# The 48 steps of the later modulation rows: one at a time, or two in a row

## The chip, the cores and the metric

The kernel runs on one core of a Trainium2 chip. The time is that of the device, in microseconds, for one launch: lower is better. A core has five engines with instruction queues of their own: TensorE (PE, its weight loads are shown as PEld), VectorE (DVE), ScalarE (ACT), GpSimd (POOL) and SyncE (SP), which here only issues transfers from the memory (HBM) into the core's SBUF. Each engine works through its instructions in the order of the program, and waits on semaphores for the others.

## The reference

One layer of a diffusion backbone: 256 latent tokens x and 256 context tokens, model width D = 2048, everything in float32.

```
mod = silu(c) @ w_mod + b_mod          # 2048 -> 6 x 2048: sh1, sc1, g1, sh2, sc2, g2
h = modulate(rms_norm(x), sh1, sc1); hc = the same for the context
p = h @ w_in; pc = hc @ w_in[:, :STATE_END]
...  # short convolutions, gated DeltaNet (8 heads, both directions) from p and pc,
...  # a Conformer convolution branch from p
x = x + g1 * rms_norm(mix @ w_out)
hf = modulate(rms_norm(x), sh2, sc2)
x = x + g2 * rms_norm((silu(hf @ w_gate) * (hf @ w_up)) @ w_down)
```

`mod` is a product of one vector with a matrix of 2048 x 12288. Its first two rows (sh1, sc1) are needed before the projections. The next three (g1, sh2, sc2) are needed only after the mixer, and they are "the later modulation rows". The last one, g2, is made on VectorE during the feed-forward part.

## The kernel before, in words

**Products.** TensorE multiplies float32 in a split form: each operand is a high part (`w_hi`) and a low part (`w_lo`), and three matmuls (high x high, high x low, low x high) make one product (helper `product`, L1775). ScalarE makes the high part by a copy (`hi` step, L921), VectorE the low part as `raw - w_hi` (`lo` step, L1355).

**Units and the ring.** Weights of the projections come in units of 128 x 1024 elements (512 KB). Each is loaded into one of four slots of `raw` (RING = 4), split into one of four slots of `w_hi` and `w_lo`, and multiplied by the `mm` step in four quarters (`QS = 4`). There are 128 units of the input projections ("win"), two small ones ("ba"), and 32 of the output projection ("wo").

**The later modulation rows.** They are worked out in 48 steps `mrm`: three row groups (MR = 3) of 16 steps (KT = 16). A step takes 128 rows of `w_mod`, 2048 columns wide, as two halves of 512 KB. Each half is loaded into a slot of the same ring `raw`, and is not split: TensorE reads it in plain float32. A step is four matmuls of 512 columns (L2083), each with one column of weights (`csil`), in four column groups of the array at once. All accumulate in PSUM bank 3. After the 16th step of a group, ScalarE copies the sums (`mrc`), and TensorE turns them (`mcol`), then VectorE adds the bias (`mcc`).

**The order of the loads.** `make_plan` writes one list of steps; every engine walks this list and does its own steps of it. At its end the list `ring` is taken from it: one entry for each `hi` step and two for each `mrm` step, in the order of the plan. Entry n uses slot n % 4. SyncE issues the loads in this order (L731), and before that of entry n it waits for the last reader of entry n - 4:

```
old = RINGED[n - RING]
if old[0] == "mr":
    need(sp, "mrm", *old[1:3])
else:
    need(sp, "hi", old)
    need(sp, "lo", old)
```

So a slot that held a modulation half is free when TensorE has done that step, and one that held a unit is free when VectorE has made its low part.

**The order around the steps.** `splits_ahead` puts the `hi` and `lo` steps of a unit two units ahead of its `mm` (AHEAD = 2). Where a level of the solver's inverse (`z`, `zc`, `xy`, `xadd`) falls into a unit, it is one unit ahead, and one more `hi` comes right behind the `zc`, one more `lo` right behind the `xadd`. In a unit, behind each quarter, the planner lays the steps of the solver, of the scan's state, of the norms and of VectorE's convolution (`dw`), by lags counted in quarters. The `mrm` steps come behind the last quarter of a unit, by the count of the units done: `gates(MR * KT * done // total - (MR * KT - len(mr)))`, with 48 steps over 108 units, so one every two or three units.

**The early rows.** The first two modulation rows are made by 32 `wm` steps in the first 127 us. They have the same shape as an `mrm` step, with two columns of weights and a buffer of their own (`first`, L1870).

Of the kernel before, what the change touches and what calls it, by code (L numbers as in the profile page):

```python
# [31 lines left out]
KT = D // P  # L32
# [29 lines left out]
MR = 3  # L62
# [105 lines left out]
def norm_chunks():  # L168

    ch = [[("lnm", ()), ("cen", ())], [("csq", (0,))]]  # L170
    ch += [[("lnv", (i,)), ("lva", (i,))] + ([("csq", (i + 1,))] if i < 3 else []) for i in range(4)]
    ch += [[("lsd", ()), ("lnr", ()), ("lnn", ())]]
    ch += [[("lny", (i,)), ("mix_hi", (NP + i,)), ("mix_lo", (NP + i,))] for i in range(4)]
    return ch


def evacuation(cu):

    what, s, p = cu
    m = NP * s + p  # L180
    if what in "kvq":
        return [("tap2", cu), ("tapa", cu)], [(AFTER["taps"][m], [("taps", cu)]), (AFTER["csilu"][m], [("csilu", cu)]), (AFTER["nat"][m], [("nat", cu), ("natc", cu)])], []
    if what == "z":
        return [("zsilu", cu)], [], []
    if what == "a":
        return [], [], []
    return [("sg", (p,)), ("u", (p,))], [], [[("dw", (p, n))] for n in range(NDW)]
# [15 lines left out]
def make_plan():  # L203
    plan = [("masks", ()), ("zero", ()), ("csil", ())]
    mr = [(grp, j) for grp in range(MR) for j in range(KT)]
# [3 lines left out]
    def put(steps):  # L209
        plan.extend(steps)  # L210
        for x in steps:
            placed[x] = slot[0]

    def unit(u, parts=1, beside=lambda: None):
        plan.extend([("hi", (u,)), ("lo", (u,))])
        for part in range(parts):
            plan.append(("mm", (u, part)))
            beside()
# [45 lines left out]
    def gates(n):  # L264
        for grp, j in mr[:n]:
            if grp and j == 0:
                plan.extend([("mcol", (grp - 1,)), ("mcc", (grp - 1,))])
            plan.append(("mrm", (grp, j)))
            if j == KT - 1:
                plan.append(("mrc", (grp,)))  # L270
        del mr[:n]
# [37 lines left out]
    done = 0  # L309
    total = 4 * (len(STREAM) - 1 - len(EARLY))  # L310
    for n, cu in enumerate(STREAM):
        if cu == ("z", LAT, NP - 1):
            gates(len(mr))
            plan.extend([("mcol", (MR - 1,)), ("mcc", (MR - 1,))])
        rest = [c[0] for c in STREAM[n:]]
        slot[2] = slot[0] + 16 * (rest.index("g") + 1 if "g" in rest else 4)
        if cu == EARLY[-1]:
            pass
        for g in range(NQ - 1 if cu in EARLY else 0, 4):
            unit(("win", cu, g), QS, beside)  # L320
            done += cu not in EARLY
            gates(MR * KT * done // total - (MR * KT - len(mr)))
            plan.extend(lat)
            del lat[:]
        now, then, later = evacuation(cu)
        put(now)
        soon += [(slot[0] + wait, steps) for wait, steps in then]
        late += later
        if cu == ("g", LAT, 3):
            late += norm_chunks()  # L330
        if n in (MIX["ba0"], MIX["ba1"]):
            s = CTX if n == MIX["ba0"] else LAT
            if cu[0] in "kvq":
                put([("taps", cu)])
                soon.remove(next(x for x in soon if x[1] == [("taps", cu)]))
            unit(("ba", s))
            put([(x, (s,)) for x in GATE_STEPS[:7]])
            soon.append((slot[0] + AFTER["gates"], [(x, (s,)) for x in GATE_STEPS[7:]]))
            soon.sort(key=lambda x: x[0])
# [80 lines left out]
def count_steps():  # L420

    plan, ring = make_plan()
    count, totals = {}, {}
    for kind, key in plan:
        assert (kind, key) not in count, (kind, key)
        totals[kind] = totals.get(kind, 0) + 1
        count[kind, key] = totals[kind]

    bank, before, reader = {}, {}, {}
    free, lent = [(6, None), (7, None)], None  # L430
    for kind, key in plan:
        if kind == "mm" and key[0][0] == "wo" and not lent:
            lent = [step for n, step in free if n == 2]
            free = [x for x in free if x[0] != 2]
            assert lent
        release = released_by(kind, key)
        if release:
            assert free, (kind, key)
            bank[kind, key], before[kind, key] = free.pop(0)
            reader[release] = bank[kind, key]  # L440
        if (kind, key) in reader:
            free.append((reader.pop((kind, key)), (kind, key)))
        if (kind, key) == ("u", (0,)):
            free.append((2, (kind, key)))
    assert not reader
    return plan, ring, count, totals, bank, before, lent[0]
# [1739 lines left out]
```

## Time and profile before

| | us |
|---|---|
| median of 3 runs | 1656.04 (1654.19 to 1660.93) |
| profiled execution, span from first to last instruction | 1654.2 |
| mean granted TensorE clock | 0.985 |
| PE busy | 1555.3 (94%) |
| DVE busy | 1043.9 (63%) |
| ACT busy | 769.0 (46%) |
| POOL busy | 226.7 (14%) |

The page of the profile gives no other time for the profiled execution than its span; the fastest of the timed runs, 1654.19 us, agrees with it. The `mrm` steps lie between 174 and 757 us. PE busy is the time covered by at least one matmul, whose ends are modelled: matmuls overlap in the records, so a matmul's own duration (0.28 us) is more than its distance to the next one (0.12 us). The distances between starts are what counts. "Idle before" in a row is the time in which the engine did nothing before the instruction, with the name of what ended it.

### The profile page before, as it was taken

The page shows a single profiled execution, that of the slowest core. Times are in us where ns is not written, and L with a number is a line of the kernel's source. Part 1 is how long each engine was busy: PE and PEld are TensorE (multiplying, and loading weights), DVE is VectorE, ACT ScalarE, POOL GpSimd, SP SyncE. Part 2 cuts the span into 40 slices and gives each one's busy share as a digit, 9 for nine tenths or more (in the row PEclk, how much of TensorE's full clock was granted, in tenths as well). Part 3 has the DMA queues.
Part 4 walks back from the last instruction along what each step waited for, and adds up shares of the span by engine and source line. Part 5 has one row for each costly group of instructions (what it writes and reads, how often), then busy time and mean ns, then how long its engine had stood idle before and what let it go on. Part 6 is the DMA issues. An engine that isn't in the chain of part 4 may idle for free.

```text
span 1654.2 us, 25093 instructions
## 1 busy us (share of the span) xinstructions
PE 1555.3 (94%) x9295; PEld 1300.8 (79%) x9295; DVE 1043.9 (63%) x1446; ACT 769.0 (46%) x1044; POOL 226.7 (14%) x236
## 2 busy tenths in 40 slices
PE   3787899998989999999998999999999999999998
PEld 0466788887879898898876888888888888888786
DVE  1445798989897957675565554444555454777554
ACT  5536543534345745456345644444444444443332
POOL 2000233323332334244200000000000000000000
PEclk9999999999999999999999999999999999999999
DMA  9994465655555556564464666666666666898653
GB/s 343 374 378 112 143 211 166 205 178 194 177 166 166 166 181 199 173 200 139 129 223 120 189 188 189 188 189 189 190 190 190 190 190 198 323 314 312 208 181 131
DMA packets 190977, 334.58 MB, mean 202 GB/s; under 512 B 14706, under 2 KB 80354, under 8 KB 189985
## 3 DMA queue, kind: packets, MB, share of 16 engines
q1 hardware_dynamic: 190194, 330.89, 62.3%
q0 software_dynamic: 688, 2.39, 0.5%
q8 instruction: 63, 1.03, 0.3%
q14 instruction: 32, 0.26, 0.1%
HBM read 331.15 MB, written 2.10 MB: 201 GB/s over the span
## 4 chain that ended last, share of the span: by engine, by line
PE 80%; DVE 10%; DMA 4%; ACT 3%; issue 2%; SPq 1%; DVEq 0%; ACTq 0%
PE PS L1775 65%; DMA first<-in_w_mod_dram 4%; DVE cacc L1636 3%; DVE w_lo L1355 2%; PE PS L1781 2%; PE PS L2083 2%; PE PS L2037 2%; PE PS L1989 2%; DVE sil L1464 1%; PE PS L1935 1%; PE PS L1870 1%; PE PS L1979 1%; DVE gh L1522 1%; DVE xyi L1527 1%; SPq L708 1%
## 5 line engine op out<-in xcount | busy, mean ns | idle before, releaser
L921 ACT ACTIVATE w_hi<-raw 128x1024 fp32r<-128x1024 f32 (+1 forms) x426 | 448.4, 1056 | 526.6 <-PE PS L1775 440.3
L1322 DVE TENSOR_TENSOR w_lo<-raw,w_hi 128x1024 fp32r<-128x1024 f32 x264 | 322.9, 1225 | 324.3 <-ACT w_hi L921 324.3
L1775 PE MATMUL PS<-w_hi,h_hi 128*128 128x512 f32 x704 | 275.0, 391 | 1.8 <-DVE h_lo L1377 1.2
L1775 PE MATMUL PS<-w_hi,h_lo 128*128 128x512 f32 x704 | 274.0, 389 | 0.0
L1775 PE MATMUL PS<-w_lo,h_hi 128*128 128x512 f32 x704 | 274.0, 389 | 0.0
L1355 DVE TENSOR_TENSOR w_lo<-raw,w_hi 128x1024 fp32r<-128x1024 f32 (+1 forms) x162 | 202.0, 1255 | 75.9 <-ACT w_hi L921 75.9
L1775 PE MATMUL PS<-h_hi,w_hi 128*128 128x256 f32 (+1 forms) x784 | 238.0, 304 | 0.8 <-ACT w_hi L921 0.8
L1775 PE MATMUL PS<-h_lo,w_hi 128*128 128x256 f32 (+1 forms) x784 | 222.1, 283 | 0.0
L1775 PE MATMUL PS<-h_hi,w_lo 128*128 128x256 f32 (+1 forms) x784 | 222.1, 283 | 0.0
L1775 PEld LDWEIGHTS PS<-h_hi,w_hi 128*128 128x128 f32 (+1 forms) x784 | 149.3, 190 | 36.9 <-issue 24.2
L1775 PEld LDWEIGHTS PS<-w_hi,h_hi 128*128 128x128 f32 x704 | 132.2, 188 | 29.5 <-DVE h_lo L1377 1.4
L1775 PEld LDWEIGHTS PS<-w_hi,h_lo 128*128 128x128 f32 x704 | 132.1, 188 | 27.6
L1775 PEld LDWEIGHTS PS<-w_lo,h_hi 128*128 128x128 f32 x704 | 132.2, 188 | 27.1
L1775 PEld LDWEIGHTS PS<-h_lo,w_hi 128*128 128x128 f32 (+1 forms) x784 | 149.6, 191 | 0.9
L1775 PEld LDWEIGHTS PS<-h_hi,w_lo 128*128 128x128 f32 (+1 forms) x784 | 149.0, 190 | 0.1
L1775 PE MATMUL PS<-w_hi,act_hi 128*128 128x512 f32 x352 | 140.4, 399 | 0.0
L1775 PE MATMUL PS<-w_hi,act_lo 128*128 128x512 f32 x352 | 139.5, 396 | 0.0
L1775 PE MATMUL PS<-w_lo,act_hi 128*128 128x512 f32 x352 | 139.5, 396 | 0.0
L1636 DVE SCALAR_TENSOR_TENSOR cacc<-ub,vcol,cacc 128x196 f32<-128x196 f32 (+14 forms) x240 | 123.9, 576 | 0.2
L870 POOL TENSOR_TENSOR mkl<-kc,lvl 128x512 fp32r<-128x512 f32 x56 | 82.4, 1471 | 158.5 <-PE PS L1979 123.8
L1775 PE MATMUL PS<-hc_hi,w_hi 128*128 128x256 f32 (+1 forms) x272 | 84.9, 312 | 12.7 <-DVE sil L1464 3.9
L1522 DVE TENSOR_TENSOR gh<-PS,side 128x1024 fp32r<-128x1024 f32 x48 | 58.5, 1219 | 43.5 <-PE PS L1989 42.5
(322 smaller groups left out, 2374.4 us busy)
## 6 DMA issues: line engine op xcount, KB each, us to landing
raw<-in_w_in_dram SPq DMA_DIRECT2D x128, 512.0 KB, 3.9
raw<-in_w_mod_dram SPq DMA_DIRECT2D x96, 512.0 KB, 4.8
raw<-in_w_gate_dram SPq DMA_DIRECT2D x88, 512.0 KB, 3.7
raw<-in_w_up_dram SPq DMA_DIRECT2D x88, 512.0 KB, 3.7
raw<-in_w_down_dram SPq DMA_DIRECT2D x88, 512.0 KB, 4.3
first<-in_w_mod_dram SPq DMA_DIRECT2D x64, 512.0 KB, 10.3
raw<-in_w_out_dram SPq DMA_DIRECT2D x32, 512.0 KB, 4.1
gin<-in_w_mod_dram SPq DMA_DIRECT2D x32, 512.0 KB, 5.8
```

The lines of the kernel that those rows point to most:

```text
L708: sp.dma_start(first[:, slot, :].rearrange("p (a b) -> p a b", a=2), w_mod_v[:, 2 * j:2 * j + 2, part * D + q * 512:part * D + (q + 1) * 5 ...
L870: pool.tensor_tensor(mkl[:, :, :, :].rearrange("p t h c -> p (t h) c"), kc[:, :, :, :].bitcast(F32).rearrange("p t h c -> p (t h) c"), bc( ...
L921: act.activation(out_ap, in_ap, ACT.Copy).then_inc(S[kind], 1)
L1322: dve.tensor_tensor(w_lo[:, slot, :], raw[:, (R0 + n) % RING, :], w_hi[:, slot, :].bitcast(F32), ALU.subtract).then_inc(S["lo"], 1)
L1355: dve.tensor_tensor(lo, raw[:, at_ring[u] % RING, 0:sz], hi.bitcast(F32), ALU.subtract).then_inc(done, 1)
L1522: dve.tensor_tensor(gh[:, :, :, :, :].rearrange("p a t h c -> p (a t h) c"), grown.rearrange("p a (n c) -> p (a n) c", c=P), bc(side[:, l, ...
L1636: ins = dve.scalar_tensor_tensor(out=dst, in0=src, scalar=vcol[:, col:col + 1], in1=dst, op0=ALU.mult, op1=ALU.add)
L1775: ins = pe.matmul(out_ap, a[i], b[j], start=start and n == 0, stop=stop and n == 2, skip_group_check=grouped)
L1781: ins = pe.transpose(PS[:, bank_, P * n:P * (n + 1)], src, ident[:, :])
L1989: ins = pe.matmul(PS[:, b, P * n:P * (n + 1)], a, m, start=False, stop=True, skip_group_check=True)
L2037: ins = pe.matmul(PS[:, b, P * n:P * (n + 1)], a, m, start=True, stop=True)
L2083: ins = pe.matmul(PS[32 * tile:32 * tile + 1, 3, :], csil[:, LAT, j:j + 1], raw[:, n % RING, 512 * h:512 * (h + 1)], start=j == 0, stop=j ...
```

## The change

The number of steps that are due after a unit is rounded to an even number: the steps are emitted two at a time, at 24 places instead of 48. The places of the second, fourth, ... step stay. The rest of the order is as it was, and so are the shapes, the buffers and the semaphores.

```
@@ -319,7 +319,7 @@
         for g in range(NQ - 1 if cu in EARLY else 0, 4):
             unit(("win", cu, g), QS, beside)
             done += cu not in EARLY
-            gates(MR * KT * done // total - (MR * KT - len(mr)))
+            gates(2 * (MR * KT // 2 * done // total) - (MR * KT - len(mr)))
             plan.extend(lat)
             del lat[:]
         now, then, later = evacuation(cu)
```

As `ring` is taken from the plan, the order of the loads follows: a pair has four entries in a row.

## Rows read from the trace of the kernel before

**Rows 1.** The page, busy time of each engine.
```profile
PE 1555.3 (94%) x9295; PEld 1300.8 (79%) x9295; DVE 1043.9 (63%) x1446; ACT 769.0 (46%) x1044; POOL 226.7 (14%) x236
```
**Rows 2.** Stretches: length, then busy PE, PEld, DVE, ACT, POOL, PEclk, DMA share, GB/s.
```profile
160.00:360.00 200.00, 186.72 (x1469) 166.49 (x1468) 176.65 (x311) 93.70 (x146) 58.43 (x53) 0.97 0.55 179
360.00:560.00 200.00, 186.62 (x1453) 166.66 (x1452) 179.76 (x296) 93.68 (x146) 63.02 (x58) 0.97 0.54 178
560.00:757.00 197.00, 192.62 (x1575) 172.95 (x1574) 131.41 (x205) 114.87 (x191) 72.68 (x75) 1.00 0.57 183
```
**Rows 3.** The page, the group of the steps' matmuls: busy, mean ns, idle before.
```profile
L2083 PE MATMUL PS<-raw,csil 128*1 128x512 f32 x384 | 51.6, 609 | 1.6 <-DMA raw<-in_w_mod_dram 1.6
```
**Rows 4.** TensorE's timeline (start, duration): steps 2, 16, 36 and 48.
```profile
188.59 1.04 PE L2083 MATMUL PS<-raw,csil 128*1 128x512 f32 x8
...
354.86 1.04 PE L2083 MATMUL PS<-raw,csil 128*1 128x512 f32 x8
...
613.17 1.04 PE L2083 MATMUL PS<-raw,csil 128*1 128x512 f32 x8
...
756.08 1.04 PE L2083 MATMUL PS<-raw,csil 128*1 128x512 f32 x8
```
**Rows 5.** TensorE's timeline around one step.
```profile
306.60 0.28 PE L1775 MATMUL PS<-h_hi,w_lo 128*128 128x256 f32 x1
306.81 1.04 PE L2083 MATMUL PS<-raw,csil 128*1 128x512 f32 x8
...
308.01 0.28 PE L1775 MATMUL PS<-h_lo,w_hi 128*128 128x256 f32 x1
```
**Rows 6.** TensorE's timeline, two early steps in a row.
```profile
71.16 1.90 PE L1870 MATMUL PS<-first,csil 128*2 128x512 f32 x16
```
**Rows 7.** SyncE's queue in the timeline, before step 16.
```profile
345.10 0.82 SPq L731 DMA_DIRECT2D raw<-in_w_mod_dram  x2
```
**Rows 8.** VectorE's timeline: low parts of the units split last before a place.
```profile
190.56 1.23 DVE L1355 TENSOR_TENSOR w_lo<-raw,w_hi 128x1024 fp32r<-128x1024 f32 x1 [0.46 <-ACT w_hi L921]
...
256.93 1.22 DVE L1355 TENSOR_TENSOR w_lo<-raw,w_hi 128x1024 fp32r<-128x1024 f32 x1
...
355.24 1.21 DVE L1522 TENSOR_TENSOR gh<-PS,side 128x1024 fp32r<-128x1024 f32 x1
356.37 1.21 DVE L1355 TENSOR_TENSOR w_lo<-raw,w_hi 128x1024 fp32r<-128x1024 f32 x1
...
381.38 1.22 DVE L1355 TENSOR_TENSOR w_lo<-raw,w_hi 128x1024 fp32r<-128x1024 f32 x1
...
753.44 1.22 DVE L1355 TENSOR_TENSOR w_lo<-raw,w_hi 128x1024 fp32r<-128x1024 f32 x1
```
**Rows 9.** The page, DMA issues: KB each, median us from issue to landing.
```profile
raw<-in_w_in_dram SPq DMA_DIRECT2D x128, 512.0 KB, 3.9
raw<-in_w_mod_dram SPq DMA_DIRECT2D x96, 512.0 KB, 4.8
```
**Rows 10.** TensorE's timeline, two idle times and what ended them.
```profile
491.70 0.84 PE L1967 MATMUL PS<-nid_r,pi 128*128 128x128 f32 x4 [2.59 <-DVE pi L1509]
...
624.04 0.66 PE L1781 MATMUL PS<-ident,sil 128*128 128x128 f32 x4 [1.42 <-ACT sil L1048]
```
**Rows 11.** Stretches behind idle times, columns as in rows 2.
```profile
249.70:256.50 6.80, 6.75 (x30) 4.92 (x31) 5.61 (x12) 1.06 (x1) 1.81 (x2) 0.50 0.67 217
...
492.00:495.50 3.50, 3.50 (x17) 3.24 (x15) 3.39 (x8) 0.00 (x0) 1.36 (x2) 0.51 0.00 0
...
624.00:627.40 3.40, 3.36 (x28) 3.27 (x29) 3.21 (x4) 3.35 (x11) 0.53 (x1) 1.00 0.20 35
```
**Rows 12.** Waits from 160 to 757 us: us in total, times, longest.
```profile
PE PS L1967 <- DVE pi L1509: 6.6, 3, 2.7
...
PE PS L1989 <- ACT pi L921: 2.5, 5, 0.8
...
ACT w_hi L921 <- DMA raw<-in_w_in_dram: 63.5, 30, 9.6
```

More of the change, by code:

```diff
@@ L321, in make_plan @@
             done += cu not in EARLY
-            gates(MR * KT * done // total - (MR * KT - len(mr)))
+            gates(2 * (MR * KT // 2 * done // total) - (MR * KT - len(mr)))
             plan.extend(lat)
```

## The prediction

> **What bounds the kernel now.** I read the busy line, then the stretches of the span, then TensorE's timeline around one step, then the DMA issues, then VectorE's timeline at the places that the change keeps. The busy line has PE at 94% [rows 1]. By stretches, PE is busy for 187 of each 200 us while the 48 modulation steps are worked in (160 to 757 us), and VectorE for 177 and 180 of 200 us up to 560 us [rows 2]. So PE sets the time, and VectorE is close behind it: whatever keeps PE waiting is paid in full, and VectorE has little room to do its work early. One core, one profiled execution: span 1654.2 us, which is 1.8 us under the median of 1656.04; I add that at the end.
>
> **The change, part by part.** Work is the same: 48 steps, 384 matmul records [rows 3], 96 loads of 512 KB. The 24 places that stay are those of the second, fourth, ... step (with 108 units counted, the j-th pair comes after unit 4.5 j rounded up, where step 2j was). The first step of each pair moves back by two or three units. I number the places 1 to 24; the first is at 188.6 us, the last at 756.1 us [rows 4].
>
> *What it saves (term A).* A step uses one column in each of four column groups of the array, the projections use all 128. Around a single step, the last matmul before starts at 306.60, the step at 306.81, and the second matmul behind it at 308.01 [rows 5]. Matmuls follow each other by 0.12 us there, so without the step that one would start at 306.84: a step costs 1.17 us. The trace of before has two such steps in a row, among the early ones: 16 records in 1.90 us against 8 in 1.04 us [rows 5, 6]. The second costs 0.86 us, which is 0.31 us less. 24 x 0.31 = 7.4 us saved, if nothing waits. Bounds: 0 (if a pair would drain between its halves, which [rows 6] exclude) and 7.4. Two smaller parts have one answer: the turning of row group 0 and 1 (mcol, mcc) moves back with the pair and has nobody waiting for it, and the copies mrc stay. Cost 0.
>
> *What it adds (term B).* The raw ring has four slots and a step takes two, each filled by a load that SyncE issues in ring order. A load may be issued only when the slot's last reader is through. Before, a step's two loads reused the slots of the step before or of the units just behind it, and were issued early: for the step at 354.86 us at 345.10 us [rows 4, 7]. Now the four loads of a pair take the whole ring. The fourth reuses the slot of the unit split last ahead of the pair, and that unit is the second one *behind* the pair on PE. So the load must wait for this unit's w_lo on VectorE (L1355), and the pair's second half waits on PE for the load. In PE's queue everything stands behind it: the projections and all the solver's matmuls.
>
> How late is that w_lo? Its end minus the place, in the trace, for the 24 places (first, last and the telling ones in between are in [rows 4, 8]): +3.2, +0.7, +0.3, -3.5, +2.7, +1.4, +1.3, +2.7, +2.0, +0.2, +1.7, +5.6, -1.5, -0.6, +2.5, -0.9, -0.3, +2.5, -2.9, 0.0, +2.5, +3.6, -1.6, -1.4 us. A load lands 3.9 us after its issue (median of the units' loads; those of the steps 4.8, since they queue in twos) [rows 9]. PE does the pair's first half meanwhile, 0.9 us. So the stall is that number + 3.0 us, where positive. It is 2 us or more at 19 of 24 places, and the sum is 93 us. PE's stalls also give VectorE and ScalarE time to catch up, so I split the 93 by what makes the w_lo late:
> - Places 8, 15, 18 and 22: in VectorE's order the w_lo stands right behind the work on the solver's last matmuls before the place (gh at 355.24, then w_lo at 356.37 [rows 8]). It is late by its position, no slack on VectorE helps. 5.7 + 5.5 + 5.5 + 6.6 = 23 us, kept in full.
> - Places 2, 9, 11, 12, 17 and 24: the same, but with one to three quarter units between. 26 us; two of them (381.38 to 382.60 at place 9 [rows 8], and place 12) carry a backlog too and are cut to 3.6 us: 20 us.
> - The other 14 (43 us, place 1 alone 6.2): the w_lo comes before the last unit in the order, and is late by backlog only. Place 4 shows it without: 256.93 to 258.15 [rows 8], 3.5 us ahead of its place, no stall. Bounds 5 and 43; between ends far apart I take about half, 23 us, as the stalls slow PE by some 15% against a VectorE that is 88% busy.
> Term B is 66 us, with bounds 40 and 93.
>
> The Trainium skill (DMA: Bandwidth & Descriptors, Anatomy of one DMA) gives a fixed 2.0 us plus the bytes at 436 GB/s, an estimate of 3.2 us for 512 KB. The trace has 3.9 [rows 9]. By the page each stall would be 0.7 us shorter and the forecast some 15 us lower; the row decides.
>
> *Clock (term C).* After PE had idled 2.59 us, ended at 491.70, the granted clock in the next 3.5 us was 0.51, the lower of its two levels (1.2 GHz); behind an idle time that ended at 249.75 us it was 0.50 for 6.8 us. Behind one of 1.42 us, at 624 us, it stayed at 1.00 [rows 10, 11]. At half clock 3.4 us of matmuls take 1.7 us more. I expect some 14 stalls over 2 us: 14 x 1.7 = 24 us, less 5 for the low stretches of before that lie where PE now waits anyway. 19 us; bounds 9 and 37 (22 stalls).
>
> *Loads of the units behind a pair (term D).* They reuse the pair's slots, and SyncE issues them in order behind the fourth load. Where PE stalls, they land about as PE goes on, and cost nothing. At the few places without a stall (4, 13, 19, 23) the first lands some 5 us after the place, and ScalarE, which splits in order, holds up its next copies: 1 to 2 us each, 5 us together; bounds 0 and 15. On the other side, the ring is free of steps between the pairs: the waits of ScalarE for loads, 63.5 us in 30 cases, in part go away. They cost PE little before (it waited 2.5 us for ScalarE's pi [rows 12]), so I count nothing.
>
> *Waits given back (term E).* PE waited for VectorE's results, 6.6 us for pi alone, 18 us over its five such groups [rows 12]. A VectorE with more time makes half of it go: -9 us; bounds 0 and -18.
>
> Sum: -7 + 66 + 19 + 5 - 9 = +74 us on 1654.2, so 1728, and with the 1.8 us 1730 us.
>
> **The rivals.**
> 1. *The loads come in time, and the saving is left:* 1656 - 7 = 1649 us, and with some of the waits of E 1645. For it: the planner's order lets a split run two units ahead, and at places 4 and 19 it is 3 us ahead of the place. Against it: it needs the fourth slot free 3 us before the place at nearly all 24, and 15 of the 24 w_lo end at or after the place. It decides if VectorE's backlog vanishes after the first stalls *and* the ten by position don't matter; the second can't be.
> 2. *Catch-up is complete:* only the places late by position stall (23 + 12 + 5 = 40 us) with 8 falls of the clock (14 - 5 = 9), -18 of E: 1656 + 40 + 9 + 2 - 18 - 7 = 1682 us. For it: w_lo takes 1.2 us and ScalarE is half idle [rows 2]. Against: VectorE's convolution work is laid between the quarter units and keeps its place beside PE.
> 3. *No catch-up:* 93 + 37 + 6 - 7 = +129, so 1785 us. For it: what VectorE does is mostly released by PE, so a stall of PE stalls it too. Against: 88% busy is not 100%.
> 4. *The pair isn't back to back:* if a bank or a sem forced the drain, A is 0 and the forecast 1737; this changes no sign.
>
> **How the numbers follow.** The forecast with its own range of 1705 to 1755 gets 0.6, rival 3 (from 1755) 0.15, rival 2 (1675 to 1705) 0.2, rival 1 0.05, of which 0.02 is below 1648. A change of 0.5% (8.3 us) is about what the measurement can tell. Rival 4 lies inside the forecast. The range for 8 in 10 leaves out the far parts of rivals 2 and 3 and all of 1: 1688 to 1768. Faster 0.02, same 0.03, slower 0.95.
>
> **What would show it.** In the changed profile: 16 records of L2083 where before there were 8, and when the loads are in, 1.9 us for them (A). PE's waits, in L2083's group: "DMA raw<-in_w_mod_dram", 1.6 us before, some 60 us in about 20 cases (B), each ended by a load issued right after a w_lo of L1355. In the windows, the granted clock of 160 to 757 us (0.97, 0.97, 1.00 before) down to about 0.95 or less (C); the stretch from the last pair on unchanged in length. The first place must show about 6 us. The prediction is wrong if PE's waits for those loads stay under 20 us, or if the fourth load turns out to be issued well ahead of the place: then the ring is not what decides.

## The result, and the profile after

The changed kernel takes 1777.44 us (median of four runs, 1775.03 to 1779.88) beside 1657.58 us for the kernel before on the same chip: 1.0727 times as long, 95% interval 1.0708 to 1.0747. The forecast was 1730 us with a range to 1768: the sign is right, the size is 47 us short, outside the range. (A timed execution is some 1.8 us longer than its span: the profiled one of the changed kernel has 1775.76 and 1774.0. So the span of 1654.2 us before belongs to the run of 1656.04, not to the fastest one.)

From the page of the changed kernel: the span, the busy line, the group of VectorE's w_lo and that of the steps' matmuls, and the two kinds of loads (median us to landing last).

```profile
span 1774.0 us, 25093 instructions
...
PE 1582.9 (89%) x9295; PEld 1319.3 (74%) x9295; DVE 1041.2 (59%) x1446; ACT 767.0 (43%) x1044; POOL 224.8 (13%) x236
...
L1355 DVE TENSOR_TENSOR w_lo<-raw,w_hi 128x1024 fp32r<-128x1024 f32 (+1 forms) x162 | 202.8, 1260 | 121.4 <-ACT w_hi L921 121.2
...
L2083 PE MATMUL PS<-raw,csil 128*1 128x512 f32 x384 | 62.1, 726 | 94.4 <-DMA raw<-in_w_mod_dram 94.3
...
raw<-in_w_in_dram SPq DMA_DIRECT2D x128, 512.0 KB, 5.0
raw<-in_w_mod_dram SPq DMA_DIRECT2D x96, 512.0 KB, 3.4
```

Of the 119.8 us that the span has grown, TensorE's idle time has 92.2 (191.1 against 98.9) and its busy time 27.6, with as many matmuls as before [rows 1]. The idle time in front of the steps' matmuls went from 1.6 us [rows 3] to 94.4. The stretches, columns as in [rows 2]:

```profile
160.00:360.00 200.00, 162.01 (x1228) 144.03 (x1226) 150.30 (x266) 83.71 (x132) 48.66 (x45) 0.92 0.47 149
360.00:560.00 200.00, 159.29 (x1214) 139.60 (x1215) 152.05 (x263) 68.70 (x106) 54.73 (x51) 0.90 0.48 153
560.00:760.00 200.00, 169.77 (x1273) 149.82 (x1272) 120.03 (x190) 94.60 (x159) 57.26 (x54) 0.93 0.46 147
760.00:877.00 117.00, 102.03 (x791) 91.13 (x787) 63.34 (x93) 54.34 (x88) 31.56 (x36) 0.93 0.48 147
877.00:1012.00 135.00, 131.93 (x714) 111.00 (x714) 77.96 (x109) 63.24 (x92) 23.29 (x24) 1.00 0.52 170
1012.00:1774.00 762.00, 746.79 (x3298) 611.64 (x3298) 416.48 (x383) 325.71 (x362) 0.00 (x0) 0.99 0.65 204
```

The whole loss lies between 160 and 877 us, where the 24 pairs are. There PE is busy for 159 to 170 of 200 us where it had 187, and its granted clock is 0.90 to 0.93 where it had 0.97 to 1.00 [rows 2]. From 877 us on, clock and busy share are high again. PE's waits over the span, longest totals first (us, times, longest):

```profile
PE PS L2083 <- DMA raw<-in_w_mod_dram: 94.3, 22, 8.3
PE PS L1870 <- DMA first<-in_w_mod_dram: 36.9, 17, 8.3
PE PS L2010 <- DVE zi L1534: 6.0, 3, 2.9
PE PS L1781 <- DVE x L1693: 5.6, 1, 5.6
PE PS L1967 <- DVE pi L1509: 5.0, 3, 2.8
```

One pair in full, the fifth. TensorE's, VectorE's and SyncE's timelines and ScalarE's around it (a bracket is the idle time before, and what ended it):

```profile
303.25 1.04 PE L2083 MATMUL PS<-raw,csil 128*1 128x512 f32 x8
309.89 1.89 PE L2083 MATMUL PS<-raw,csil 128*1 128x512 f32 x8 [5.60 <-DMA raw<-in_w_mod_dram]
```
```profile
304.67 1.26 DVE L1355 TENSOR_TENSOR w_lo<-raw,w_hi 128x1024 fp32r<-128x1024 f32 x1
305.85 3.31 DVE L1636 SCALAR_TENSOR_TENSOR cacc<-ub,vcol,cacc 128x244 f32<-128x244 f32 x8
317.60 1.23 DVE L1522 TENSOR_TENSOR gh<-PS,side 128x1024 fp32r<-128x1024 f32 x1 [8.43 <-PE PS L1989]
```
```profile
303.79 2.54 SPq L731 DMA_DIRECT2D raw<-in_w_mod_dram  x2
306.39 5.82 SPq L731 DMA_DIRECT2D raw<-in_w_in_dram  x3
```
```profile
315.31 0.60 ACT L921 ACTIVATE kn<-PS 128x512 f32<-128x512 f32 x1 [13.36 <-PE PS L1781]
```

The w_lo of the unit split last ends at 305.93, the second of the two loads on SyncE's queue goes out right behind it (the row holds both), and TensorE's second step starts at 309.89, 4.0 us after the w_lo. This is the chain that the prediction gave. What it did not give is on the other two engines: VectorE works until 309.16 and then stands 8.4 us for a matmul of the solver (L1989) that is queued behind the second step, and ScalarE stands 13.4 us for TensorE. They don't use TensorE's wait; they share it. VectorE's waits for L1989 before its `gh`, in the stage of the steps (160 to 757 us before, 160 to 877 after), have doubled:

```profile
DVE gh L1522 <- PE PS L1989: 36.0, 19, 4.1
```
```profile
DVE gh L1522 <- PE PS L1989: 72.0, 18, 10.5
```

(The second step takes 1.89 us where a step took 1.04: the trace's clock record has the lower level, 0.5, from 308.1 us on for 6.8 us.)

### The profile page after: what moved, and what is told of

The parts are those of the page before. It is cut to its first block, busy times and chain, and to the rows that moved or that the text cites. A ratio compares the mean times of both kernels' runs of the same rounds, so it can differ in the third digit from the quotient of the medians.

```text
span 1774.0 us, 25093 instructions
## 1 busy us (share of the span) xinstructions
PE 1582.9 (89%) x9295; PEld 1319.3 (74%) x9295; DVE 1041.2 (59%) x1446; ACT 767.0 (43%) x1044; POOL 224.8 (13%) x236
## 4 chain that ended last, share of the span: by engine, by line
PE 69%; DVE 15%; DMA 8%; issue 4%; ACT 2%; SPq 2%; POOL 1%; DVEq 0%; ACTq 0%; POOLq 0%
PE PS L1775 57%; DMA raw<-in_w_mod_dram 4%; DVE w_lo L1355 4%; DVE cacc L1636 3%; DMA first<-in_w_mod_dram 3%; DVE sil L1464 2%; PE PS L2083 2%; PE PS L1781 2%; DVE gh L1522 2%; SPq L708 2%; PE PS L1989 1%; PE PS L2037 1%; DMA raw<-in_w_in_dram 1%; PE PS L1935 1%; ACT w_hi L921 1%
## 5 line engine op out<-in xcount | busy, mean ns | idle before, releaser
L1775 PE MATMUL PS<-h_hi,w_hi 128*128 128x256 f32 (+1 forms) x784 | 244.1, 311 | 1.2 <-DVE ub L1616 1.2
L1775 PE MATMUL PS<-h_lo,w_hi 128*128 128x256 f32 (+1 forms) x784 | 227.6, 290 | 0.0
L1775 PE MATMUL PS<-h_hi,w_lo 128*128 128x256 f32 (+1 forms) x784 | 227.3, 290 | 0.0
L1775 PEld LDWEIGHTS PS<-h_hi,w_hi 128*128 128x128 f32 (+1 forms) x784 | 155.6, 199 | 30.6 <-issue 29.9
L1775 PEld LDWEIGHTS PS<-h_lo,w_hi 128*128 128x128 f32 (+1 forms) x784 | 155.9, 199 | 1.0
L1775 PEld LDWEIGHTS PS<-h_hi,w_lo 128*128 128x128 f32 (+1 forms) x784 | 154.8, 197 | 0.1
L2083 PE MATMUL PS<-raw,csil 128*1 128x512 f32 x384 | 62.1, 726 | 94.4 <-DMA raw<-in_w_mod_dram 94.3
```

Source lines behind the costliest of these rows:

```text
L1775: ins = pe.matmul(out_ap, a[i], b[j], start=start and n == 0, stop=stop and n == 2, skip_group_check=grouped)
L2083: ins = pe.matmul(PS[32 * tile:32 * tile + 1, 3, :], csil[:, LAT, j:j + 1], raw[:, n % RING, 512 * h:512 * (h + 1)], start=j == 0, stop=j ...
```

## The experiments

Eleven more kernels were run. The last four columns are read from each one's trace between 160 and 880 us: TensorE's waits for the steps' loads, the sum of its other waits, ScalarE's waits for the units' loads at its copies, and the time for which the trace's clock records have the lower level (records that start between 150 and 880 us).

| kernel | us | to before | interval | steps' loads | other PE waits | ACT for units | low clock |
|---|---|---|---|---|---|---|---|
| before | 1654.7 to 1657.6 | 1 | | 1.6 | 32 | 63.5 | 24 |
| after | 1777.4 | 1.0727 | 1.0708 to 1.0747 | 94.3 | 30 | 98.6 | 116 |
| zero_single | 1656.5 | 0.9996 | 0.998 to 1.0012 | 0 | 35 | none | 20 |
| zero_pair | 1657.3 | 1.0010 | 0.9994 to 1.0026 | 0 | 39 | none | 24 |
| two | 1654.3 | 0.9992 | 0.9978 to 1.0006 | 0 | 37 | 21.4 | 24 |
| three | 1696.8 | 1.0251 | 1.0220 to 1.0282 | 9.1 | 55 | 87.5 | 55 |
| zero_hold | 1737.6 | 1.0503 | 1.0476 to 1.0530 | 0 | 27 | none | 7 |
| fill | 1749.9 | 1.0568 | 1.0540 to 1.0596 | 27.2 | 32 | 97.9 | 24 |
| apart | 1686.5 | 1.0182 | 1.0150 to 1.0213 | 23.1 | 30 | 56.3 | 44 |
| odd | 1768.4 | 1.0672 | 1.0635 to 1.0709 | 72.0 | 39 | 120.6 | 123 |
| light | 1752.4 | 1.0585 | 1.0560 to 1.0611 | 78.9 | 23 | 91.9 | 113 |
| halfway | 1727.1 | 1.0438 | 1.0418 to 1.0458 | 35.1 | 52 | 121.7 | 65 |
| six | 1667.7 | 1.0078 | 1.0061 to 1.0095 | 5.5 | 39 | 77.0 | 24 |

**Without loads: zero_single and zero_pair.** From the kernel before and the changed one:

```
-    ring = [u for kind, key in plan if kind in ("hi", "mrm")
-            for u in ([key[0]] if kind == "hi" else [("mr", *key, 0), ("mr", *key, 1)])]
+    ring = [key[0] for kind, key in plan if kind == "hi"]
...
-                                        raw[:, n % RING, 512 * h:512 * (h + 1)], start=j == 0, stop=j == KT - 1)
+                                        h_hi[:, 4 * half + 2 * h:4 * half + 2 * h + 2, :].bitcast(F32).rearrange("p a b -> p (a b)"),
+                                        start=j == 0, stop=j == KT - 1)
```

> The kernel before, but its 96 loads for the later modulation rows are left out and the steps multiply a tensor that stays in SBUF; the ring holds the units' loads alone. It is the base for zero_pair. All theories: PE's waits for these loads (1.6 us before) are gone, ScalarE's waits for loads at its copies (63.5 us before) fall. PE's other waits, 27 us before, may fall a little: 1650 us, between 1640 and 1658.

> The changed kernel with the same edit: the 24 pairs of steps stand where the change puts them, but need no load and take no slot of the ring. Theory (the ring decides: the fourth load of a pair waits for the w_lo of the unit split last): all of the 94 us of waits and the half-clock time go with it, and what is left is the saving of 0.31 us for each pair, so 7.4 us under zero_single, about 1643 us. Rival (two steps in a row hurt by themselves, by what VectorE and the solver wait for while PE works on a pair): it stays above zero_single, by 10 us or more. If a pair drains between its halves: equal to zero_single within 1.5 us.

zero_single takes 1656.5 us, within its range, but TensorE's other waits did not fall (35 us for 32). Without loads the pairs cost nothing: the 120 us come with the loads and the slots that they take. But the saving of 7.4 us isn't there either: the two differ by 0.8 us the wrong way, with intervals of 2.6 us each side. The profiled executions show where most of it went. TensorE's busy time is 5.2 us shorter (1557.2 and 1552.0), its other waits are 4 us longer, and its whole idle time 3.0. The two groups of waits for VectorE that grew most, in zero_single, then in zero_pair:

```profile
PE PS L1780 <- DVE kn L1477: 6.5, 3, 2.6
PE PS L2009 <- DVE zi L1533: 5.7, 3, 2.4
```
```profile
PE PS L1780 <- DVE kn L1477: 8.3, 4, 2.9
PE PS L2009 <- DVE zi L1533: 7.6, 4, 2.8
```

Most of what TensorE saves it waits for VectorE: by 3.7 us more in these two groups, by 3.9 over all its waits for VectorE (that for pi fell from 6.6 to 4.2). The last expectation of zero_pair (equal, if a pair drains between its halves) holds in its number but not in its reason: two steps with their data in start 0.86 us apart, in the changed kernel too (fourth pair, 16 records in one row):

```profile
276.20 1.90 PE L2083 MATMUL PS<-raw,csil 128*1 128x512 f32 x16
```

The Trainium skill (TensorEngine Tiling (Array Packing), Key Properties) says that a change of the tiling mode drains the engine. The trace fits it: [rows 5, 6] put 0.31 us on one visit to the one-column tiles. That these 0.31 us are such a drain, no run here shows; the section gives no figure.

**How many slots: two and three.** The second step reads slots of the first, so fewer are loaded:

```
+def halves(key):                       # three; in two the list for odd steps is empty
+    return [("mr", *key, 0)] if key[1] % 2 else [("mr", *key, 0), ("mr", *key, 1)]
...
-                        n = at_ring["mr", grp, j, half]
+                        n = at_ring["mr", grp, j, 0 if j % 2 else half]
```

> The changed kernel, but the second step of each pair reads the two slots of the first: 48 loads of 512 KB are left out, and a pair takes two slots of the ring, as a single step did before. The last load then reuses the slot of the unit split three ahead, whose w_lo is done 3 us or more before the place everywhere in the trace of before. Ring theory: PE's waits for these loads stay under 8 us, 1650 us (1645 to 1660). Rival (it is the later place of the first step's loads or the burst on the queue, not the slot): waits stay above 40 us.

> The changed kernel, but the second step of each pair reads its first half's slot twice: 24 loads of 512 KB are left out, and a pair takes three slots. Its last load reuses the slot of the unit split last but one ahead of the pair. From the w_lo of that unit in the trace of before (its end minus the place, plus 3.0 us, where positive) the waits add up to 9 us, at six places (1, 3, 5, 6, 7, 14). Ring theory: PE waits 5 to 15 us for these loads, the clock costs 3 us, 1662 us (1653 to 1672). Rival (the number of bytes or of queued loads ahead of a pair decides, so the waits shrink in proportion to the loads): one quarter to one half of the 94 us is left at 15 or more places, 1700 us or above.

With two slots to a pair the loss is gone. With three, the waits for the loads are as the rule has them, 9.1 us at six places (9.2 forecast), but the kernel is 41 us slower: my 1662 was wrong by 35. Against two, TensorE's idle time is 27 us longer (126.7 and 99.3) and its busy time 17. Only 9 of the 27 are at the pairs. ScalarE's waits for the units' loads, in two and in three:

```profile
ACT w_hi L925 <- DMA raw<-in_w_in_dram: 21.4, 11, 5.3
```
```profile
ACT w_hi L925 <- DMA raw<-in_w_in_dram: 87.5, 24, 11.9
```

A pair with three or four slots leaves a ring with nothing loaded behind it. ScalarE's next copy of a unit then waits for a load that could start only after the pair's, and what ScalarE owes TensorE (pi, sil) is queued behind that copy. TensorE's waits for the two, in two and in three:

```profile
PE PS L1993 <- ACT pi L925: 3.4, 6, 0.9
PE PS L1785 <- ACT sil L1052: 0.4, 1, 0.4
```
```profile
PE PS L1993 <- ACT pi L925: 9.7, 9, 4.2
PE PS L1785 <- ACT sil L1052: 5.4, 3, 4.7
```

This is term D, which I had put at 5 us. In the changed kernel no sum shows it beside the pair's own wait.

**Hold TensorE without taking slots: zero_hold.** From zero_pair:

```
-                    for tile in range(4):
-                        half, h = divmod(tile, 2)
+                    for tile in range(4 + 20 * (j % 2)):
+                        again, tile = divmod(tile, 4)
+                        half, h = divmod(tile, 2)
```

> zero_pair (no loads for the steps), with the second step of each pair multiplied six times: TensorE is kept busy 4.3 us more at each of the 24 places, 103 us in all (5 x 0.86 us x 24), which is what the waits of the changed kernel come to (94 us), but no slot of the ring is taken. It asks why VectorE did not catch up during the waits. Theory 1 (after a pair the ring is empty, so ScalarE and with it VectorE stand still): here they catch up; the w_lo of the last unit ends 2 us or more sooner against the place than in zero_pair at the places late by backlog, TensorE's other waits (38.6 us between 160 and 800 us in zero_pair) fall by a third or more, and the time is 1657 + 103 - 15 = 1745 us. Theory 2 (VectorE's work is released by TensorE, so it stands still with it): lateness unchanged within 1 us, waits unchanged, 1760 us.

Each theory was right in one half. The lateness of the w_lo (its end minus the place) is unchanged, to 0.15 us at 22 of 24 places against zero_pair; and at 20 of 24 it is the same as in the changed kernel. So VectorE does not catch up at the places: at the fifth it stands 4.64 us for TensorE's L1988 (the line called L1989 elsewhere), where it had stood 8.43.

```profile
297.85 1.28 DVE L1354 TENSOR_TENSOR w_lo<-raw,w_hi 128x1024 fp32r<-128x1024 f32 x1
299.05 3.31 DVE L1635 SCALAR_TENSOR_TENSOR cacc<-ub,vcol,cacc 128x244 f32<-128x244 f32 x8
307.01 1.22 DVE L1521 TENSOR_TENSOR gh<-PS,side 128x1024 fp32r<-128x1024 f32 x1 [4.64 <-PE PS L1988]
```

The time, though, is 1737.6 and not 1760: of some 100 us of hold about 20 come back. TensorE's idle time is 15 us shorter than in zero_pair (88.8 and 103.8; other waits 27 us against 39), and the low-clock time falls from 24 to 7 us. The changed kernel gets less of this. Its other waits are 30 us, 9 less than in zero_pair but only 2 less than in the kernel before. ScalarE shows a difference, at the seventh place of zero_hold and of the changed kernel:

```profile
351.50 0.60 ACT L1168 ACTIVATE sgb<-PS 128x512 f32<-128x512 f32 x1 [8.63 <-PE PS L1774]
351.99 1.05 ACT L920 ACTIVATE w_hi<-raw 128x1024 fp32r<-128x1024 f32 x1
```
```profile
363.86 0.60 ACT L1169 ACTIVATE sgb<-PS 128x512 f32<-128x512 f32 x1 [8.63 <-PE PS L1775]
370.34 1.06 ACT L921 ACTIVATE w_hi<-raw 128x1024 fp32r<-128x1024 f32 x1 [5.88 <-DMA raw<-in_w_in_dram]
```

With units in the ring the copy starts at once; behind a pair of four slots it waits 5.9 us and starts 1.4 us after TensorE's second step (368.96), for which TensorE had waited 4.2 us.

**The clock alone: fill.** From the changed kernel, with R from 0 to 8 by place, 81 in all:

```
+                    if j % 2:
+                        for again in range(R[(KT * grp + j) // 2]):
+                            for tile in range(4):
+                                pe.matmul(PS[32 * tile:32 * tile + 1, 3, :], csil[:, LAT, j - 1:j],
+                                          h_hi[:, 2 * tile:2 * tile + 2, :].bitcast(F32)..., start=False, stop=False)
```

> The changed kernel with filler: ahead of the second step's wait TensorE multiplies a tensor that stays in SBUF, 0 to 8 times 0.86 us at each place, so many as fit its measured wait less about 1 us (82 times in all, 71 us; the modulation rows come out changed). Nothing else moves. It measures the clock's part alone. Theory: the low-clock time of 160 to 880 us, 116 us against 24 before, is made by the idle times, so it goes back to some 30 us, and the time falls by 25 to 30 us to 1750 us. Rival (fillers of one column each don't keep the clock, or the clock falls for another reason): 1777 us and the low-clock time stays above 90 us.

As expected: 1749.9 us. The ratios differ by 0.0159, which is 26 us. The waits are only filled, not shortened (81 x 0.86 us of filler and the 27.2 us that are left make 97 us), so the 26 us are the clock's. The stretch 160 to 360 us of fill has the granted clock at 0.96, where the changed kernel has 0.92:

```profile
160.00:360.00 200.00, 181.22 (x1436) 151.04 (x1434) 153.22 (x271) 84.04 (x132) 51.33 (x46) 0.96 0.49 151
```

**Other places: apart and odd.** All work is done; only the places change:

```
-            gates(2 * (MR * KT // 2 * done // total) - (MR * KT - len(mr)))
+            gates(MR * KT // 2 * done // total + MR * KT // 2 * max(0, done - 1) // total - (MR * KT - len(mr)))   # apart
+            gates(2 * ((MR * KT * done // total + 1) // 2) - (MR * KT - len(mr)))   # odd
```

> All work as in the changed kernel and 24 places for the first steps where it has them, but the second step of each pair stands one unit later. Then no place needs four slots of the ring at once. Ring theory: its loads reuse the slots of the first step, issued right after it, and land some 5 us later, about when TensorE reaches the second step (a unit takes 5 to 6 us of projections and what lies between): waits under 20 us, 1660 us (1652 to 1675). Rival (the loads queued for two steps so near each other hurt in any case, since the units' loads queue behind them): 1700 us or more.

> The changed kernel with the pairs at the places of the odd steps (1, 3, 5, ...) in place of the even ones; all work is done. The rule (end of the w_lo of the unit split last, minus the place, plus 3.0 us, where positive, from the trace of the kernel before) gives 71 us of waits at these 24 places, where it gave 93 at the others; the largest at the 9th pair (7.2), none at pairs 1, 15, 18 and 23. Theory: waits of 65 to 78 us, three quarters of the clock's cost, 1745 us (1735 to 1760). Rival (which unit comes ahead does not matter): 1777 us again, with waits of 90 us or more.

odd bears the rule out in the sum of 24 other places: 72.0 us of waits for a forecast of 71. Single places are off by up to 2.4 us either way, so that the sum comes so near is in part luck. Its time was missed by 23 us, since the rest grew: the low clock is on for 123 us, ScalarE stands 121 us for units, and TensorE's other waits are 9 us more. apart was missed by 26 us. The loads of its second step come 2 us too late at 12 places (23.1 us); so it isn't the four slots alone. What fits is that a load which waits for a slot needs some 4 us until it can be used; no run tests that by itself.

**VectorE's part: light.**

```
+                    if n:
+                        taps = taps[-1:]
...
-                        for h in range(2):
+                        for h in range(2) if n == 0 else [1]:
```

> The changed kernel with most of the convolution's taps on VectorE left out (of each run of them but the first pair one of every two to eight stays; no other instruction changes). So far the w_lo of the last unit ends at the same time against the place in every kernel, to 0.1 us at most places, also where TensorE was held 4.3 us at each place: VectorE gained nothing. Theory: what stands in VectorE's order between its last step released by TensorE and the w_lo sets the lateness, at the 14 places called backlog too; taps stand there, so without them these w_lo end 1 to 3 us sooner: waits of 50 to 70 us instead of 94 (the 23 us at places 8, 15, 18, 22, with no taps between, stay within 2 us). Rival (the lateness comes from TensorE or the loads, not from VectorE's work): waits of 85 us or more.

Between the two: 78.9 us. At places 8, 15, 18 and 22 the lateness stays within 0.3 us (2.5, 2.5, 2.5 and 3.6), and it falls by 1.0 to 2.3 us at places 5, 7, 9, 10, 12 and 14, where taps stand ahead of the w_lo. At 20 and 21 it stays at +1.3 and +2.5; what sets it there no run shows. VectorE is busy for 119 of 200 us (160 to 360 us) where it was for 150, and the mean lateness of the 14 places goes from +0.4 to -0.3 us, that of the six from +1.5 to +0.5. So its work counts, but with a fifth of it gone five sixths of the waits remain.

**All work, and the pair later on TensorE: halfway.** The plan moves each pair but the last past two quarter units and holds the next unit's split until it:

```
+        if pair and (step[0] != "mm" or step[1][1] == 2 or step[0] == "mm" and step[1][0][0] != "win"):
+            if step[0] == "mm":
+                rest += pair
+                pair = []
```

> All work, the changed kernel with each pair of steps but the last two quarter units later on TensorE (between the second and the third quarter of the next unit), in the same order in the ring and with the next unit's split still behind it. TensorE has 2.6 us of projections more before it needs the loads; of the measured waits (98 us in 24 places) what is over 2.6 us adds up to 46. Theory: waits of 35 to 60 us, half of the clock's 27 us; but the loads of the units behind the pair come no sooner, so ScalarE still stands some 90 us for them and TensorE's other waits rise by 10 to 20 us: 1727 us (1705 to 1745). Rival (only the wait at the pair costs, nothing behind it): under 1705 us. Rival (moving it gives nothing, since VectorE's order moves with TensorE): 1770 us or more.

1727.1 us is the forecast, in part by luck: the waits, 35 us, are at the low end of theirs, while ScalarE's waits for units rose to 121.7 us (for some 90) and TensorE's other waits by 22 us to 52 (for 10 to 20). Moving the pair cuts the first cost and feeds the second.

```profile
ACT w_hi L943 <- DMA raw<-in_w_in_dram: 121.7, 34, 9.0
...
PE PS L2105 <- DMA raw<-in_w_mod_dram: 35.1, 11, 7.0
```

**Only the six easy places: six.**

```
+            n1 = MR * KT * done // total
+            n1 -= n1 % 2 and (n1 + 1) // 2 in (4, 13, 16, 19, 23, 24)
+            gates(n1 - (MR * KT - len(mr)))
```

> All work, pairs at six of the 24 places only (4, 13, 16, 19, 23 and 24, where the w_lo ended 1 to 3 us before the place), the other 36 steps single as in the kernel before. Waits at these six in the changed kernel: 0, 1.1, 0.3, 0.4, 1.4, 1.4 us. If nothing but the wait at the pair costs: 1655 + 5 - 6 x 0.31 = 1658 us. If an empty ring behind the pair also costs where TensorE does not wait for the steps' loads (in the kernel with three slots to a pair 9 us of such waits came with 41 us, so some 1.3 us a place): 1666 us.

1667.7 us: 0.8% slower with only 5.5 us of waits for the steps' loads, near the second theory's 1666 and not the first's 1658. Of the 12 us by which the profiled execution is longer, 7 are idle time of TensorE; 4 of the 5 us of busy time lie ahead of 160 us, where there are no pairs. At the fourth place nothing waits at the pair, and ScalarE's next copy of a unit comes 3.4 us late:

```profile
261.50 1.90 PE L2085 MATMUL PS<-raw,csil 128*1 128x512 f32 x16
```
```profile
262.11 1.14 ACT L923 ACTIVATE mhi<-mn 128x512 fp32r<-128x512 f32 x2
266.61 1.06 ACT L923 ACTIVATE w_hi<-raw 128x1024 fp32r<-128x1024 f32 x1 [3.36 <-DMA raw<-in_w_in_dram]
```

No version here beats the kernel before. The most that pairs gave in any run is the 1.5 us of two, which leaves half of the steps' loads out, with an interval that holds no change.

## Why the prediction was wrong in size

The sign, the stage, the chain at the ring and the first place (5.6 us for "about 6") were right; that VectorE would catch up was not. By terms, forecast and measured:

- **B, the ring: +66, measured +93** (94.3 less 1.6; 98 us if at each of the 24 places the distance between the two steps' starts is taken less 0.86 us). This is the step that failed, and it has 27 of the 47 us. The naive sum of 93 was right; the cut for "catch-up" was not. By class, in the count that gives 98: positional places 23 forecast and 23.0 measured; the six next to them 20 and 26.8; the other 14, halved from 43 to 23, 48.6. I took the lateness at those 14 for a backlog that idle time on TensorE would work off. zero_hold shows that holding TensorE for 100 us leaves it where it is, and odd that the rule's sum holds uncut elsewhere (72.0 for 71). VectorE waits for matmuls queued behind the waiting step (gh for L1989: 36.0 us before, 72.0 after), so it starts again with TensorE. That its own order then makes the lateness anew fits light in part: at places such as 20 and 21 the cause stays open.
- **C, the clock: +19, measured +26** (fill). The unit cost was sound; 18 waits over 2 us came where I counted 14, because B was cut. TensorE's busy time rose by 27.6 us.
- **E, waits given back: -9, measured -2** against the kernel before (30 us for 32). Against zero_pair, which has the pairs and no waits for loads, it is -9 (30 for 39), so the effect is there; but the pairs had first added most of that. zero_hold, with units in the ring behind the pair, gives back more (39.4 to 26.5 us of such waits, 15 us of idle time). A and E together were -16 in the sum and near 0 in the time.
- **A, the saving: -7.4, measured about 0** (zero_pair against zero_single, +0.8; two against before, -1.5). TensorE did save 5 us of busy time in zero_pair, and waited most of it out on VectorE. And where the pair is split by a wait there is no second step in a row.
- **D, loads of the units behind: +5.** In the changed kernel it isn't seen beside B. As a mechanism it was far undersized: six takes 12.6 us more, of which 3.9 are waits for the steps' loads at its pairs, and three 41 us, of which 9.1 are; the rest in three includes what the clock adds (55 us at the lower level, before 24).

Measured: 93 + 26 - 2 = +117, beside 119.8 us on the span; the other 3 us stand in no term.

Two readings of rows were off as well, with no effect on the sum. 16 of the 24 w_lo end at or after their place, not 15. And the 2.0 us plus bytes at 436 GB/s are given in the Trainium skill (DMA: Bandwidth & Descriptors, Anatomy of one DMA) for the GpSimd path, while the loads here go out on SyncE's queue; their 3.9 us [rows 9] say nothing against it.

Rival 3, no catch-up, had the reason: what VectorE does is mostly released by TensorE. Its 1785 us came near by some luck, as its clock term was 11 us too high and its saving of 7 us did not come. It got 0.15, against "88% busy is not 100%". That argument counts busy time; the question was what VectorE waits for. The row was there: between 160 and 757 us of the kernel before, VectorE's gh waited 36.0 us for L1989, in 19 cases.

## What to carry to other kernels

When an in-order engine is made to wait, first ask which of the others' next instructions depend on something queued behind the wait: they stop with it, and here a lateness that was read in the trace before stayed as it was at most places. A group of operations that fills a ring of buffers was paid for twice here, by its own last load and by the first users behind it, so compare slots needed with slots there before looking at queue order. And a saving of 5 us on the busiest engine was worth nothing here, with VectorE busy for some 88% of the time up to 560 us [rows 2] and TensorE waiting for it in turn.

## What the runs showed of the hardware

Idle times filled with one-column matmuls, which use one column in each of four column groups, left TensorE at the clock of the kernel before: 24 us at the lower level in fill, 24 in the kernel before and 116 in the changed one. In zero_hold, where such matmuls stand at every place, it is 7 us.

Median landing times differ between the two kernels with the same sizes and the loads in another order: a step's load 4.8 us before [rows 9] and 3.4 after, a unit's 3.9 and 5.0. In the changed kernel the last load of a pair lands 3.6 us after its issue (median of 24), and the units' two loads behind it, issued 0.4 and 0.9 us later at the fifth pair (306.39 and 306.86), take 4.8 and 5.7 (medians).
